# Feature-major x beside token-major x: the first layer's stationary tiles without transposes

## The chip, the cores and the metric

One core of a Trainium2 chip runs the kernel. The metric is the device time of one execution in microseconds, as the median over runs; smaller is better. Engines are named as in the profile: PE (TensorE; PEld its weight loads), DVE (VectorE), ACT (ScalarE), POOL (GpSimd) and SP (SyncE, which here only issues DMAs). POOL issues DMAs too, on a queue of its own.

## The reference

256 tokens of width 2048 pass through two blocks of two layers each, in float32. Only the start of the first block's first layer matters here:

```python
def hybrid_layer(x, layer_idx, norm_gain, w_in, ...):
    h = rms_norm(x, norm_gain)                      # x * rsqrt(mean(x^2) + eps) * gain
    proj = jnp.einsum('bsd,de->bse', h, w_in)       # 256x2048 @ 2048x20480
    (da_q, da_k, da_v, da_z, sb_q, sb_k, sb_v, sb_z, gate_a, gate_b) = split_columns(proj)
    q = rope(rms_norm(da_q.reshape(b, s, 2 * DA_HEADS, DA_QK_DIM), qk_q_gain))
    k = rope(rms_norm(da_k.reshape(b, s, 2 * DA_HEADS, DA_QK_DIM), qk_k_gain))
    ...                                             # two attentions, gated branches
    return x + jnp.einsum('bsd,de->bse', y, w_out)
```

The second block (a convolution, a windowed attention and a linear recurrence per layer) and everything after the first half unit of the first layer keep their instructions.

## The kernel before, in words

**Products.** Every large matrix product is made in three fp32r matmuls (hi times hi, lo of the weight, lo of the activation: lines 1955 to 1957). The weights stream from HBM once, in halves of 128 x 1024 float32 (512 KB). A half lands in one of the `RING = 4` slots of `raw`; ACT copies it to `w_hi` (line 663), DVE subtracts to `w_lo` (line 1181) and counts `split_ready`, and PE multiplies it, 12 matmuls of 512 columns for a half. I call the half with number s *weight half s* and its twelve matmuls *product s*. Eight halves make a unit of 512 output columns: products 0 to 7 fill accumulators 0 and 1, products 8 to 15 fill 2 and 3, product 16 starts the next unit. ACT may overwrite a slot of `w_hi` only when the product four back is done; SP issues the load into a slot of `raw` when `split_ready` says that the half four back was split (line 463).

**The stationary side.** `hT` holds x times the norm gain, feature-major, as hi and lo. The row factor rsqrt(mean x^2) is not in it; it is applied to the accumulators afterwards. x comes token-major in eight parts of 256 KB, 256 features each (`x_part`, line 449). For part f, PE turns four 128x128 squares with `turn_h` (line 1981) into PSUM `work`, ACT writes `hT` hi (`h_hi`, line 682) and DVE `hT` lo (`h_lo`, line 1187). In the first layer PE warms up with six matmuls on zeros (line 1990), turns parts 0 and 1, and then turns part s + 2 behind product s.

**Queues.** Each engine does its instructions in program order. SP issues: x part 0, the identity (`cst`, 64 KB), `kept` (18 KB: norm gains), then weight halves 0 to 3 alternating with x parts 1 to 4, then x parts 5 to 7, then the weight halves from 4 on as slots come free. POOL waits until all x parts are there, then issues the other constants (`cst`, 704 KB), `par` (640 KB) and the rotary tables `ropeC` and `ropeS` (256 KB each).

**What follows in the first step.** On ACT, `first_step` splits halves 8 and 9, squares x over whole rows (line 711, two instructions with a row sum each; their output goes to the scratch `rows`), splits halves 10 and 11, and then waits for POOL's row factor (`x_rstd`) before it takes the first unit's q and k out of the accumulators (`evac_qk`, line 737). On POOL, `layer_start` multiplies the tables by the gains (line 504), waits for the sums of squares and makes the row factor (lines 483 and 489); then `rotate` squares, scales and rotates q and k into `QN` (lines 515 to 533). On PE, `turn_qk` (line 2018) stands behind product 16 and waits for `QN`.

Of the kernel before, what the change touches and what calls it, by code (L numbers as in the profile page):

```python
# [28 lines left out]
ACT = mybir.ActivationFunctionType  # L29
# [142 lines left out]
        return [self.sem(f"{name}{i}") for i in range(n)]  # L172


def build_program(nc, weights, x_in, consts1, params1, kept1, rope1, meta_in, ln_in, consts2, params2,
                  mats2, rows2, out):
    with ExitStack() as ctx:
        mem = Memory(nc, ctx)
# [31 lines left out]
        SM = mem.place("SM", [P, 2, 384])  # L210
        MX = mem.place("MX", [P, 2, 384])
        rows = mem.place("rows", [P, NT, D], at=rows_at)
        pair_at = mem.at
        TZ = mem.place("TZ", [P, NT, 256])
        ZG = mem.place("ZG", [P, NT, 256])
# [32 lines left out]

        x_loaded = sems("x_loaded", 8)
        set_loaded, cst_loaded, par_loaded = sem("set_loaded"), sem("cst_loaded"), sem("par_loaded")
        first_hi, first_lo = sem("first_hi"), sem("first_lo")
        const_set, scale_due = sem("const_set"), sem("scale_due")
# [98 lines left out]
        post_delta, post_ss, post_var, post_sub, post_mul = (  # L353
            sem(n) for n in ("post_delta", "post_ss", "post_var", "post_sub", "post_mul"))
        norm_root, norm_rs, post_sqsum = sem("norm_root"), sem("norm_rs"), sem("post_sqsum")
        out_copied, out_copied2, out_stored = sem("out_copied"), sem("out_copied2"), sem("out_stored")

        def conv_tap(eng, l, ch, j):

# [85 lines left out]
        @block.sync  # L445
        def _(sp):
            def x_part(f):
                c = slice(256 * f, 256 * f + 256)
                sp.dma_start(X[:, :, c], x_in[:, c].rearrange("(t p) n -> p t n", p=P)).then_inc(x_loaded[f], 16)

            x_part(0)
            sp.dma_start(cst[:, C_ID:C_ID + P], consts1[:, C_ID:C_ID + P]).then_inc(set_loaded, 16)
            sp.dma_start(kept[:, :, :], kept1).then_inc(set_loaded, 16)
            for slot in range(RING):
                sp.dma_start(raw[:, slot, :], weights[slot]).then_inc(raw_loaded[slot], 16)
                x_part(slot + 1)
            for f in range(RING + 1, 8):
                x_part(f)
            with sp.Fori(1, n_halves // RING) as r:
                for slot in range(RING):  # L460

                    sp.wait_ge(split_ready, RING * r + (slot + 1 - RING))
                    sp.dma_start(raw[:, slot, :], weights[bass.ds(RING * r + slot, 1), :, :].rearrange("a p n -> p (a n)"))\
                      .then_inc(raw_loaded[slot], 16)

            for n, (t, j) in enumerate(OUT_ORDER):
                sp.wait_ge(out_copied2, n + 1)
                sp.dma_start(out[t * P:t * P + P, columns_of(j)], out_rows[:, t, columns_of(j)]).then_inc(out_stored, 16)
            sp.wait_ge(out_stored, 8 * 16)
# [3 lines left out]
        def _(pool):  # L473
            pool.memset(half_neg, -0.5).then_inc(const_set, 1)
            for f in range(8):
                pool.wait_ge(x_loaded[f], 16)
            pool.dma_start(cst[:, P:C_COLS], consts1[:, P:C_COLS]).then_inc(cst_loaded, 16)

            def scale(*operands):

# [10 lines left out]
            def layer_start(l):  # L491

                pool.wait_ge(y_ready, 4 * l)
                pool.dma_start(par[:, :], params1[l]).then_inc(par_loaded, 16)
                pool.dma_start(ropeC[:, :, :, :], rope1[0]).then_inc(par_loaded, 16)
                pool.dma_start(ropeS[:, :, :, :], rope1[1]).then_inc(par_loaded, 16)
                pool.wait_ge(const_set, 2)
                pool.wait_ge(par_loaded, 48 * (l + 1))
                pool.wait_ge(set_loaded, 32)

                for t in range(NT):
                    for c, table in enumerate((ropeC, ropeS)):
                        gains = par[:, R_QK + 2 * P * c:R_QK + 2 * P * (c + 1)].rearrange("p (a n) -> p a n", a=2)
                        pool.tensor_tensor(table[:, t, :, :], table[:, t, :, :], gains, ALU.mult).then_inc(tables_ready, 1)
                scale(subln[:, :], par[:, R_SUBLN:R_SUBLN + 256], kept[:, l, KC + 1:KC + 2], None,
                                   ALU.mult).then_inc(tables_ready, 1)
                pool.wait_ge(x_ss, 2 * (l + 1))
                rsqrt_mean(rstdx, ssx, x_tmp, D, tables_ready, 6 * (l + 1), x_rstd)
                pool.wait_ge(x_rstd, 2 * l + 1)
                scale(half_rstdx, rstdx, 0.5, None, ALU.mult).then_inc(x_rstd, 1)  # L510
# [138 lines left out]
        def _(act):  # L649
# [27 lines left out]
                act.activation(w_hi[:, slot, :], raw[:, slot, :], ACT.Copy).then_inc(hi_ready, 1)  # L677

            def h_hi(l, f):
                act.wait_ge(hT_turned, 8 * l + f + 1)  # L680
                for c in (2 * f, 2 * f + 1):
                    ins = act.activation(hT[0][:, c, :], work[:, f % 4, c % 2 * SEQ:(c % 2 + 1) * SEQ], ACT.Copy,
                                         scale=kept[:, l, c:c + 1])
                ins.then_inc(hT_hi, 1)

            def layer_start(l):
                u = UNITS1 * l
                if l == 0:
                    act.wait_ge(const_set, 2)
                    act.activation(small[:, 90:91], U[:, 0, 0:1], ACT.Copy)  # L690
                    act.wait_ge(set_loaded, 32)
                    act.wait_ge(raw_loaded[0], 16)
                    act.activation(w_hi[:, 0, 0:512], raw[:, 0, 0:512], ACT.Copy).then_inc(first_hi, 1)
                    h_hi(l, 0)
                    act.activation(w_hi[:, 0, 512:HALF], raw[:, 0, 512:HALF], ACT.Copy).then_inc(hi_ready, 1)
                    for f in range(1, 8):
                        split(u, f, f + 1)
                        h_hi(l, f)
                else:
                    split(u, 0, 6)  # L700
                    h_hi(l, 6)
                    h_hi(l, 7)
                    split(u, 6, 8)

            def first_step(m):
                l = m["l"]
                u = UNITS1 * l
                split(u, 8, 10)
                act.wait_ge(x_added, 4 * l)
                for t in range(NT):  # L710
                    act.activation(rows[:, t, :], X[:, t, :], ACT.Square, accum_out=ssx[:, t:t + 1]).then_inc(x_ss, 1)
                split(u, 10, 12)
                act.wait_ge(x_rstd, 2 * l + 2)
                evac_qk(m)
                split(u, 12, 14)
                act.wait_ge(lam_dots, 2 * (l + 1))
                act.activation(lam_exp, lam_dot, ACT.Exp).then_inc(lam_exps, 1)
                if l == 0:
                    act.wait_ge(cst_loaded, 16)
                    act.activation(tri[:, :], cst[:, C_NEGTRI:C_NEGTRI + 2 * P], ACT.Copy)  # L720
                split(u, 14, 16)
# [452 lines left out]
        def _(dve):  # L1174
# [9 lines left out]
            def h_lo(l, f):  # L1184
                dve.wait_ge(hT_hi, 8 * l + f + 1)
                for c in (2 * f, 2 * f + 1):
                    ins = dve.scalar_tensor_tensor(  # L1187
                        hT[1][:, c, :], work[:, f % 4, c % 2 * SEQ:(c % 2 + 1) * SEQ],
                        kept[:, l, c:c + 1], hT[0][:, c, :], ALU.mult, ALU.subtract)
                ins.then_inc(hT_lo, 1)  # L1190

            def layer_start(l):
                u = UNITS1 * l
                if l == 0:
                    dve.memset(U[:, :, :], 0.0).then_inc(const_set, 1)
                    dve.wait_ge(set_loaded, 32)
                    dve.wait_ge(first_hi, 1)
                    dve.tensor_tensor(w_lo[:, 0, 0:512], raw[:, 0, 0:512], w_hi[:, 0, 0:512], ALU.subtract).then_inc(first_lo, 1)
                    h_lo(l, 0)
                    dve.wait_ge(hi_ready, 1)  # L1200
                    dve.tensor_tensor(w_lo[:, 0, 512:HALF], raw[:, 0, 512:HALF], w_hi[:, 0, 512:HALF], ALU.subtract)\
                        .then_inc(split_ready, 1)
                    for f in range(1, 8):
                        split(u, f, f + 1)
                        h_lo(l, f)
                else:
                    split(u, 3, 6)
                    h_lo(l, 6)
# [733 lines left out]
        def _(pe):  # L1942
# [26 lines left out]

            def turn_h(l, f):  # L1970

                if l:
                    pe.wait_ge(x_added, 4 * (l - 1) + f // 2 + 1)
                else:
                    pe.wait_ge(x_loaded[f], 16)
                if f >= 4:
                    pe.wait_ge(hT_lo, 8 * l + (f - 3))
                for c in (2 * f, 2 * f + 1):
# [5 lines left out]
            def first_step(m):  # L1984
                l = m["l"]
                u = UNITS1 * l
                if l == 0:
                    pe.wait_ge(const_set, 2)
                    for _ in range(FIRST_WARM):
                        pe.matmul(work[:, 3, 0:256], U[:, 0, 0:P], U[:, 1, :], start=True, stop=True)  # L1990
                    pe.wait_ge(set_loaded, 32)
                    turn_h(l, 0)
                    turn_h(l, 1)

                pe.wait_ge(qk_evac, m["n"])
                for s in range(8):
                    halves(u, hT, s, s + 1, (hT_lo, 8 * l), l == 0 and s == 0)
                    if l == 0 and s < 6:
                        turn_h(l, s + 2)
                    if l and s == 1:  # L2000
                        turn_h(l, 6)
                        turn_h(l, 7)
# [704 lines left out]
```

## Time and profile before

| | before |
|---|---|
| device time, median of 3 runs | 3218.58 us (3218.3 to 3219.7) |
| profiled execution, span from first to last instruction | 3216.8 us |
| PE busy | 3208.1 us |
| DVE, ACT, POOL busy | 2002.6, 1666.2, 502.8 us |
| DMA, mean over the span | 177 GB/s, of 568.95 MB |

The profile is of one execution. Its span stands 1.8 us under the median of the timed runs, and within 0.1% of it. Starts are counted from the first instruction. "Idle before" is the time an engine stood still ahead of an instruction, with what released it; a DMA's "us to landing" counts from its issue until its data is there. PE's matmuls overlap their neighbours, so of two in a row the distance of the starts is what counts.

### The profile page before, as it was taken

Reading aid. Unit: us, or ns where it says so; the run is one execution under the profiler, and the core shown is the slowest. Engines: PE = TensorE matmul, PEld = TensorE weight load, DVE = VectorE, ACT = ScalarE, POOL = GpSimd, SP = SyncE. Lnnn points to the kernel's source line nnn. Section 1 sums busy time; section 2 is a strip of 40 time slices with the busy share of each in tenths; the row PEclk is TensorE's granted clock in tenths of the full one; section 3 lists DMA queues with packets and bytes.
Section 4 is the critical chain, followed back from the end, with each engine's and each line's share of the span. In section 5 each row is a group of like instructions: output and inputs, shape, how many; then the busy total and the mean of one; then the engine's idle time right before and its main releaser. Section 6 shows DMA issues by size and latency. Waiting matters only on the chain.

```text
span 3216.8 us, 47383 instructions
## 1 busy us (share of the span) xinstructions
PE 3208.1 (100%) x16986; PEld 2760.8 (86%) x16986; DVE 2002.6 (62%) x2267; ACT 1666.2 (52%) x2326; POOL 502.8 (16%) x425
## 2 busy tenths in 40 slices
PE   9999999999999999999999999999999999999999
PEld 7888888888888888888888888888889999999997
DVE  6667655555544555666654555444458888688975
ACT  5445455555444444454455555444446557465663
POOL 4544500000000003445410000000001000100000
PEclk9999999999999999999999999999999999999999
DMA  6555555554555555455555455555564444544454
GB/s 241 174 171 183 173 174 169 176 171 168 191 195 192 193 196 185 164 187 171 170 178 179 165 175 174 183 192 194 192 209 166 155 144 147 181 160 162 145 182 146
DMA packets 157289, 568.95 MB, mean 177 GB/s; under 512 B 17552, under 2 KB 19744, under 8 KB 156768
## 3 DMA queue, kind: packets, MB, share of 16 engines
q1 hardware_dynamic: 155680, 558.00, 52.1%
q0 software_dynamic: 1488, 9.26, 0.8%
q8 instruction: 86, 1.41, 0.2%
q14 instruction: 35, 0.29, 0.0%
HBM read 565.09 MB, written 2.10 MB: 176 GB/s over the span
## 4 chain that ended last, share of the span: by engine, by line
PE 99%; POOL 1%; DVE 0%; issue 0%; ACT 0%; DVEq 0%; POOLq 0%; ACTq 0%
PE acc L1955 23%; PE acc L1957 23%; PE acc L1956 23%; PE acc L2343 5%; PE acc L2344 5%; PE acc L2345 5%; PE acc L2270 1%; PE acc L2268 1%; PE acc L2269 1%; PE work L2018 1%; PE work L2406 1%; PE work L2314 1%; PE work L2317 1%; PE work L2318 1%; PE work L2373 0%; PE work L2432 0%
## 5 line engine op out<-in xcount | busy, mean ns | idle before, releaser
L1181 DVE TENSOR_TENSOR w_lo<-raw,w_hi 128x1024 fp32r<-128x1024 f32 x1055 | 1400.2, 1337 | 992.2 <-ACT w_hi L663 858.4
L663 ACT ACTIVATE w_hi<-raw 128x1024 fp32r<-128x1024 f32 x831 | 873.4, 1057 | 903.9 <-PE acc L1957 898.7
L1955 PE MATMUL acc<-w_hi,hT_hi 128*128 128x512 f32 x2560 | 1013.7, 396 | 1.4 <-DVE hT_lo L1187 1.4
L1957 PE MATMUL acc<-w_hi,hT_lo 128*128 128x512 f32 x2560 | 998.1, 390 | 0.0
L1956 PE MATMUL acc<-w_lo,hT_hi 128*128 128x512 f32 x2560 | 996.6, 389 | 0.0
L1957 PEld LDWEIGHTS acc<-w_hi,hT_lo 128*128 128x128 f32 x2560 | 480.5, 188 | 102.6
L1955 PEld LDWEIGHTS acc<-w_hi,hT_hi 128*128 128x128 f32 x2560 | 481.0, 188 | 96.2 <-issue 1.7
L1956 PEld LDWEIGHTS acc<-w_lo,hT_hi 128*128 128x128 f32 x2560 | 481.4, 188 | 95.5
L677 ACT ACTIVATE w_hi<-raw 128x1024 fp32r<-128x1024 f32 x224 | 236.1, 1056 | 260.1 <-PE acc L2345 200.1
L2343 PE MATMUL acc<-h_hi,w_hi 128*128 128x272 f32 (+1 forms) x1088 | 318.5, 293 | 0.0
L2344 PE MATMUL acc<-h_lo,w_hi 128*128 128x272 f32 (+1 forms) x1088 | 311.9, 287 | 0.0
L2345 PE MATMUL acc<-h_hi,w_lo 128*128 128x272 f32 (+1 forms) x1088 | 311.8, 287 | 0.0
L2343 PEld LDWEIGHTS acc<-h_hi,w_hi 128*128 128x128 f32 x1088 | 205.3, 189 | 2.3 <-issue 0.3
L2344 PEld LDWEIGHTS acc<-h_lo,w_hi 128*128 128x128 f32 x1088 | 205.4, 189 | 0.8
L2345 PEld LDWEIGHTS acc<-h_hi,w_lo 128*128 128x128 f32 x1088 | 205.7, 189 | 0.0
L1955 PE MATMUL acc<-w_hi,uaT_hi 128*128 128x512 f32 x512 | 200.8, 392 | 0.0
L1957 PE MATMUL acc<-w_hi,uaT_lo 128*128 128x512 f32 x512 | 199.4, 390 | 0.0
L1956 PE MATMUL acc<-w_lo,uaT_hi 128*128 128x512 f32 x512 | 199.3, 389 | 0.0
L483 POOL TENSOR_SCALAR ZG<-TZ 128x512 f32<-128x512 f32 x32 | 34.3, 1072 | 713.0 <-ACT TZ L731 713.0
L483 POOL TENSOR_SCALAR small<-small 128x8 f32<-128x8 f32 (+2 forms) x64 | 34.2, 534 | 547.7 <-ACT SM L780 339.7
L1957 PEld LDWEIGHTS acc<-w_hi,uaT_lo 128*128 128x128 f32 x512 | 96.1, 188 | 20.2
L1956 PEld LDWEIGHTS acc<-w_lo,uaT_hi 128*128 128x128 f32 x512 | 96.2, 188 | 19.6
(381 smaller groups left out, 3830.4 us busy)
## 6 DMA issues: line engine op xcount, KB each, us to landing
raw<-weights SPq DMA_DIRECT2D x1056, 512.0 KB, 3.4
mat<-mats POOLq DMA_DIRECT2D x2, 1536.0 KB, 8.7
X<-x_in SPq DMA_DIRECT2D x8, 256.0 KB, 8.1
GB_rows<-rows POOLq DMA_DIRECT2D x1, 2048.0 KB, 9.9
out<-out_rows SPq DMA_DIRECT2D x8, 256.0 KB, 2.6
par<-params POOLq DMA_DIRECT2D x2, 640.0 KB, 5.4
cst<-consts POOLq DMA_DIRECT2D x1, 704.0 KB, 6.2
cst<-consts POOLq DMA_DIRECT2D x1, 552.0 KB, 5.1
```

The lines of the kernel that those rows point to most:

```text
L483: return pool.tensor_scalar(*operands)
L663: act.activation(w_hi[:, slot, :], raw[:, slot, :], ACT.Copy).then_inc(hi_ready, 1)
L677: act.activation(w_hi[:, slot, :], raw[:, slot, :], ACT.Copy).then_inc(hi_ready, 1)
L1181: dve.tensor_tensor(w_lo[:, s % RING, :], raw[:, s % RING, :], w_hi[:, s % RING, :], ALU.subtract)\
L1955: pe.matmul(o, stat[0][:, kc, token], hi, start=(kc == 0), stop=False)
L1956: pe.matmul(o, stat[0][:, kc, token], lo, start=False, stop=False)
L1957: ins = pe.matmul(o, stat[1][:, kc, token], hi, start=False, stop=(kc == KC - 1))
L2018: ins = pe.transpose(work[:, a // 2, o:o + P], src[:, t, a, :], ident)
L2268: pe.matmul(o, y_hi, hi, start=False, stop=False, skip_group_check=True)
L2343: pe.matmul(o, hi, x_hi, start=(kc == 0), stop=False)
L2344: pe.matmul(o, hi, x_lo, start=False, stop=False)
L2345: ins = pe.matmul(o, lo, x_hi, start=False, stop=(kc == KC - 1))
```

## The change

x is given twice: as before, and as `xT_in`, the same numbers feature-major. `XT` is a tile for it, 16 KB a partition, at the address of the scratch `rows`. The first layer's `h_hi` and `h_lo` read `XT` in SBUF instead of `work` in PSUM, and the 32 transposes of that layer go. SP's order becomes: XT part 0, `kept`, weight halves 0 to 3 alternating with XT parts 1 to 4, XT parts 5 to 7, and then each of weight halves 4 to 7 with two token-major x parts behind it; from half 8 on it is as before. The identity is no longer loaded by itself: all of `cst` (768 KB) is loaded by POOL, behind `par`, `ropeC` and `ropeS`. POOL waits for the XT parts instead of the x parts. ACT's squares of the first layer wait for all of x and for the last `h_lo`, since they write over `XT`. On ACT and DVE each `h_hi` and `h_lo` comes ahead of the split of the weight half that it goes with, not behind it. The second layer and the second block keep their instructions.

```diff
+        XT = mem.place("XT", [P, KC, SEQ], at=rows_at)
...
-            x_part(0)
-            sp.dma_start(cst[:, C_ID:C_ID + P], consts1[:, C_ID:C_ID + P]).then_inc(set_loaded, 16)
+            def xT_part(f):
+                sp.dma_start(XT[:, 2 * f:2 * f + 2, :], xT_in[:, 2 * f:2 * f + 2, :]).then_inc(xT_loaded[f], 16)
+
+            def load(first, slot):
+                sp.wait_ge(split_ready, first + (slot + 1 - RING))
+                sp.dma_start(raw[:, slot, :], weights[bass.ds(first + slot, 1), :, :].rearrange("a p n -> p (a n)"))\
+                  .then_inc(raw_loaded[slot], 16)
+
+            xT_part(0)
             sp.dma_start(kept[:, :, :], kept1).then_inc(set_loaded, 16)
             for slot in range(RING):
                 sp.dma_start(raw[:, slot, :], weights[slot]).then_inc(raw_loaded[slot], 16)
-                x_part(slot + 1)
+                xT_part(slot + 1)
             for f in range(RING + 1, 8):
-                x_part(f)
-            with sp.Fori(1, n_halves // RING) as r:
+                xT_part(f)
+            for slot in range(RING):
+                load(RING, slot)
+                x_part(2 * slot)
+                x_part(2 * slot + 1)
+            with sp.Fori(2, n_halves // RING) as r:
...
             for f in range(8):
-                pool.wait_ge(x_loaded[f], 16)
-            pool.dma_start(cst[:, P:C_COLS], consts1[:, P:C_COLS]).then_inc(cst_loaded, 16)
+                pool.wait_ge(xT_loaded[f], 16)
...
                 pool.dma_start(ropeS[:, :, :, :], rope1[1]).then_inc(par_loaded, 16)
+                if l == 0:
+                    pool.dma_start(cst[:, :], consts1).then_inc(cst_loaded, 16)
...
             def h_hi(l, f):
-                act.wait_ge(hT_turned, 8 * l + f + 1)
+                if l == 0:
+                    act.wait_ge(xT_loaded[f], 16)
+                else:
+                    act.wait_ge(hT_turned, 8 * (l - 1) + f + 1)
                 for c in (2 * f, 2 * f + 1):
-                    ins = act.activation(hT[0][:, c, :], work[:, f % 4, c % 2 * SEQ:(c % 2 + 1) * SEQ], ACT.Copy,
-                                         scale=kept[:, l, c:c + 1])
+                    src = work[:, f % 4, c % 2 * SEQ:(c % 2 + 1) * SEQ] if l else XT[:, c, :]
+                    ins = act.activation(hT[0][:, c, :], src, ACT.Copy, scale=kept[:, l, c:c + 1])
...
                     for f in range(1, 8):
+                        h_hi(l, f)
                         split(u, f, f + 1)
-                        h_hi(l, f)
...
-                act.wait_ge(x_added, 4 * l)
+                if l:
+                    act.wait_ge(x_added, 4 * l)
+                else:
+                    act.wait_ge(x_loaded, 8 * 16)
+                    act.wait_ge(hT_lo, 8)
...
-                    pe.wait_ge(set_loaded, 32)
-                    turn_h(l, 0)
-                    turn_h(l, 1)
 
                 pe.wait_ge(qk_evac, m["n"])
                 for s in range(8):
                     halves(u, hT, s, s + 1, (hT_lo, 8 * l), l == 0 and s == 0)
-                    if l == 0 and s < 6:
-                        turn_h(l, s + 2)
```

DVE's `h_lo` and its place change in the same way as ACT's `h_hi`.

## Rows read from the trace of the kernel before

**Rows 1.** The page: span, and busy time of each engine.

```profile
span 3216.8 us, 47383 instructions
PE 3208.1 (100%) x16986; PEld 2760.8 (86%) x16986; DVE 2002.6 (62%) x2267; ACT 1666.2 (52%) x2326; POOL 502.8 (16%) x425
```

**Rows 2.** Waits of PE over the span: us in total, times, longest.

```profile
PE work L1990 <- DVE U L1195: 1.5, 1, 1.5
PE acc L1955 <- DVE hT_lo L1187: 1.4, 1, 1.4
PE work L2018 <- POOL QN L533: 1.0, 1, 1.0
```

**Rows 3.** The chain that ended last, 28 to 64 us: start, us, what.

```profile
28.61 0.45 PE work L1981 x4
...
29.92 1.89 ACT w_hi L663 x2
31.82 0.06 ACT rows L711
...
37.00 0.92 POOL small L483
...
60.01 1.09 PE work L2018 x8
```

**Rows 4.** Timeline, SP and POOL issues: start, us, what, idle before.

```profile
1.24 0.46 SPq L452 DMA_DIRECT2D cst<-consts  x1
2.22 0.43 SPq L455 DMA_DIRECT2D raw<-weights  x1
...
5.42 0.49 SPq L455 DMA_DIRECT2D raw<-weights  x1
...
17.79 0.68 POOL L477 DMA_DIRECT2D cst<-consts  x1 [16.94 <-DMA X<-x_in]
...
22.84 0.33 SPq L463 DMA_DIRECT2D raw<-weights  x1
```

**Rows 5.** DMA issues, us to landing: weight halves 0, 3 and 9.

```profile
raw<-weights SPq DMA_DIRECT2D x1, 512.0 KB, 4.1
raw<-weights SPq DMA_DIRECT2D x1, 512.0 KB, 8.7
raw<-weights SPq DMA_DIRECT2D x1, 512.0 KB, 6.9
```

**Rows 6.** DMA totals of two stretches: 0 to 10, then 10 to 28 us.

```profile
DMA packets 1488, 2.25 MB, mean 225 GB/s; under 512 B 242, under 2 KB 1155, under 8 KB 1488
DMA packets 2873, 7.15 MB, mean 397 GB/s; under 512 B 264, under 2 KB 1527, under 8 KB 2872
```

**Rows 7.** Timeline, DVE and ACT, splits of weight halves 0 and 1.

```profile
7.17 0.69 DVE L1198 TENSOR_TENSOR w_lo<-raw,w_hi 128x512 fp32r<-128x512 f32 x1 [5.76 <-ACT w_hi L693]
9.33 1.06 ACT L663 ACTIVATE w_hi<-raw 128x1024 fp32r<-128x1024 f32 x1 [0.23 <-DMA raw<-weights]
10.42 1.23 DVE L1181 TENSOR_TENSOR w_lo<-raw,w_hi 128x1024 fp32r<-128x1024 f32 x1 [0.33 <-ACT w_hi L663]
```

**Rows 8.** Timeline, PE: warm-up, products 0 and 1, a later matmul pair.

```profile
1.46 5.49 PE L1990 MATMUL work<-U 128*128 128x256 f32 x12 [1.46 <-DVE U L1195]
9.59 0.47 PE L1955 MATMUL acc<-w_hi,hT_hi 128*128 128x512 f32 x1 [1.45 <-DVE hT_lo L1187]
...
12.19 0.40 PE L1957 MATMUL acc<-w_hi,hT_lo 128*128 128x512 f32 x1
...
12.78 0.47 PE L1955 MATMUL acc<-w_hi,hT_hi 128*128 128x512 f32 x1
...
66.42 0.59 PE L2026 MATMUL work<-QT 128*128 128x256 f32 x2
```

**Rows 9.** Timeline, POOL: first multiplication of the tables, start of the row factor.

```profile
29.09 0.74 POOL L504 TENSOR_TENSOR ropeC<-ropeC,par 128x256 f32<-128x256 f32 x1 [9.01 <-issue]
...
35.80 0.19 POOL L483 TENSOR_SCALAR small<-small 128x2 f32<-128x2 f32 x1 [0.98 <-ACT rows L711]
```

More of the change, by code:

```diff
@@ L172, in sems, with build_program @@
         return [self.sem(f"{name}{i}") for i in range(n)]
-def build_program(nc, weights, x_in, consts1, params1, kept1, rope1, meta_in, ln_in, consts2, params2,
+def build_program(nc, weights, x_in, xT_in, consts1, params1, kept1, rope1, meta_in, ln_in, consts2, params2,
                   mats2, rows2, out):
@@ L241, in build_program @@
         assert mem.at <= 229376, mem.at
-        x_loaded = sems("x_loaded", 8)
+        xT_loaded, x_loaded = sems("xT_loaded", 8), sem("x_loaded")
         set_loaded, cst_loaded, par_loaded = sem("set_loaded"), sem("cst_loaded"), sem("par_loaded")
@@ L355, in build_program @@
         norm_root, norm_rs, post_sqsum = sem("norm_root"), sem("norm_rs"), sem("post_sqsum")
-        out_copied, out_copied2, out_stored = sem("out_copied"), sem("out_copied2"), sem("out_stored")
+        out_copied2, out_stored = sem("out_copied2"), sem("out_stored")
         def conv_tap(eng, l, ch, j):
@@ L448, in x_part @@
                 c = slice(256 * f, 256 * f + 256)
-                sp.dma_start(X[:, :, c], x_in[:, c].rearrange("(t p) n -> p t n", p=P)).then_inc(x_loaded[f], 16)
-            x_part(0)
-            sp.dma_start(cst[:, C_ID:C_ID + P], consts1[:, C_ID:C_ID + P]).then_inc(set_loaded, 16)
+                sp.dma_start(X[:, :, c], x_in[:, c].rearrange("(t p) n -> p t n", p=P)).then_inc(x_loaded, 16)
+            def xT_part(f):
[5 more added lines that the diff above has]
+            xT_part(0)
             sp.dma_start(kept[:, :, :], kept1).then_inc(set_loaded, 16)
@@ L455, in _ @@
                 sp.dma_start(raw[:, slot, :], weights[slot]).then_inc(raw_loaded[slot], 16)
-                x_part(slot + 1)
+                xT_part(slot + 1)
             for f in range(RING + 1, 8):
-                x_part(f)
-            with sp.Fori(1, n_halves // RING) as r:
+                xT_part(f)
[4 more added lines that the diff above has]
+            with sp.Fori(2, n_halves // RING) as r:
                 for slot in range(RING):
-                    sp.wait_ge(split_ready, RING * r + (slot + 1 - RING))
-                    sp.dma_start(raw[:, slot, :], weights[bass.ds(RING * r + slot, 1), :, :].rearrange("a p n -> p (a n)"))\
-                      .then_inc(raw_loaded[slot], 16)
+                    load(RING * r, slot)
             for n, (t, j) in enumerate(OUT_ORDER):
@@ L496, in layer_start @@
                 pool.dma_start(ropeS[:, :, :, :], rope1[1]).then_inc(par_loaded, 16)
+                if l == 0:
+                    pool.dma_start(cst[:, :], consts1).then_inc(cst_loaded, 16)
                 pool.wait_ge(const_set, 2)
                 pool.wait_ge(par_loaded, 48 * (l + 1))
-                pool.wait_ge(set_loaded, 32)
+                pool.wait_ge(set_loaded, 16)
                 for t in range(NT):
@@ L690, in layer_start @@
                     act.activation(small[:, 90:91], U[:, 0, 0:1], ACT.Copy)
-                    act.wait_ge(set_loaded, 32)
+                    act.wait_ge(set_loaded, 16)
+                    h_hi(l, 0)
                     act.wait_ge(raw_loaded[0], 16)
                     act.activation(w_hi[:, 0, 0:512], raw[:, 0, 0:512], ACT.Copy).then_inc(first_hi, 1)
-                    h_hi(l, 0)
                     act.activation(w_hi[:, 0, 512:HALF], raw[:, 0, 512:HALF], ACT.Copy).then_inc(hi_ready, 1)
                     for f in range(1, 8):
+                        h_hi(l, f)
                         split(u, f, f + 1)
-                        h_hi(l, f)
                 else:
@@ L1186, in h_lo @@
                 for c in (2 * f, 2 * f + 1):
-                    ins = dve.scalar_tensor_tensor(
-                        hT[1][:, c, :], work[:, f % 4, c % 2 * SEQ:(c % 2 + 1) * SEQ],
-                        kept[:, l, c:c + 1], hT[0][:, c, :], ALU.mult, ALU.subtract)
+                    src = work[:, f % 4, c % 2 * SEQ:(c % 2 + 1) * SEQ] if l else XT[:, c, :]
+                    ins = dve.scalar_tensor_tensor(hT[1][:, c, :], src, kept[:, l, c:c + 1], hT[0][:, c, :], ALU.mult, ALU.subtract)
                 ins.then_inc(hT_lo, 1)
@@ L1195, in layer_start @@
                     dve.memset(U[:, :, :], 0.0).then_inc(const_set, 1)
-                    dve.wait_ge(set_loaded, 32)
+                    dve.wait_ge(set_loaded, 16)
+                    h_lo(l, 0)
                     dve.wait_ge(first_hi, 1)
                     dve.tensor_tensor(w_lo[:, 0, 0:512], raw[:, 0, 0:512], w_hi[:, 0, 0:512], ALU.subtract).then_inc(first_lo, 1)
-                    h_lo(l, 0)
                     dve.wait_ge(hi_ready, 1)
@@ L1203, in layer_start @@
                     for f in range(1, 8):
+                        h_lo(l, f)
                         split(u, f, f + 1)
-                        h_lo(l, f)
                 else:
@@ L1970, in turn_h @@
             def turn_h(l, f):
[L1972 to L1975, printed above, removed]
+                pe.wait_ge(x_added, 4 * (l - 1) + f // 2 + 1)
                 if f >= 4:
@@ L2686 @@
         "x_in": a["x"][0],
+        "xT_in": a["x"][0].reshape(SEQ, KC, P).transpose(2, 1, 0),
         "consts1": stack1_consts(),
```

## The prediction

> **What bounds the kernel now.** I read the page first. PE is busy for 3208.1 of 3216.8 us [rows 1], so only 8.7 us of the span can be taken from its pauses, and everything else has to come out of its own instructions. The list of PE's waits says where the pauses are: three in the whole execution, all in the first 60 us: 1.5 us before the warm-up, 1.4 us before product 0 (for `hT` lo), and 1.0 us at `turn_qk` for `QN` from POOL [rows 2]. Behind that third one PE waits for nobody until the end. So the question for any edit of the start is a single one: when does PE get past `turn_qk`, at 60.0 us now? A shift there moves the end one to one.
>
> The chain of waits answers what sets the 60.0 us, and it is not PE. Followed from 28.6 us, it leaves PE at the transposes of x part 7, goes to ACT (`hT` hi of part 7, then the splits of weight halves 8 and 9, 29.92 to 31.81 us), to ACT's squares of x at 31.82, to POOL's row factor, done at 37.9, through `evac_qk` and the rotation to `QN`, and back to PE at 60.01 [rows 3]. From the start of the squares to `turn_qk` this is 28.2 us of ACT, POOL and DVE work, none of which the change touches. PE reaches `turn_qk` at 59.0 and waits 1.0.
>
> Third, the DMA totals: from 10 to 28 us the queues moved 7.15 MB at 397 GB/s; in the 10 us before that, 2.25 MB at 225 GB/s [rows 6]. The start of this kernel fills the DMA engines until weight half 9 lands, issued at 22.84 and landing 6.9 us later, at 29.7 [rows 4, 5].
>
> **What is removed.** Six groups of four transposes stood between products. One group costs the distance from the last matmul of product 0 to the first of product 1, 12.78 - 12.19 = 0.59 us, less the 0.23 us that two matmuls of a product stand apart: 0.36 us, so 2.2 us for six. The first two groups stood ahead of product 0, which now waits only for weight half 0 and `hT` of part 0. Half 0 landed at 2.22 + 4.1 = 6.3 us [rows 4, 5] and its first 512 columns were split at 7.17 + 0.69 = 7.9 [rows 7]; the identity's issue ahead of it took 0.5 us of SP's time [rows 4] and goes, so 7.4. Product 0 starts at 7.4 instead of 9.59 [rows 8], 2.2 us earlier. With weights always at hand PE would be 4.4 us ahead: product 5 done at 7.4 + 6 x 2.73 = 23.8 us, product 7 at 29.2 (12 matmuls by 0.2275 us are 2.73).
>
> **What is added.** 2.10 MB. x is still loaded whole, and XT comes ahead of it. Both stand before weight half 8 on SP's queue, and none of it is in a gap: the stretch to 28 us is full. The cost of the eight x parts, from two sides: at the full rate, 2.10 MB / 397 GB/s = 5.3 us; by what x parts took, weight half 3 landed at 5.42 + 8.7 = 14.1 [rows 4, 5], and POOL, which waits for the last x part, went on at 17.79 [rows 4], so four parts behind it took at most 3.7 us, 0.9 each, 7.2 for eight. I take the middle, 6.2. Against it stand two gains. An XT part has rows of 2 KB where an x part has 1 KB; the trace shows no such transfer, it lies between the x part (0.9 us) and the full rate (0.66 us for 256 KB), so eight save 0 to 1.9 us; I take 0.8. And weight half 0 is issued 0.5 us earlier, of which I take 0.4. Weight half 9, which landed at 29.7, then lands at 29.7 + 6.2 - 0.8 - 0.4 = 34.7 us. The lower bound is 29.7 + 5.3 - 1.9 - 0.5 = 32.6, and if the whole slow start to 10 us should go faster as well (2.25 MB at 397 GB/s take 5.7 us, and the first data can't land before 3 us; at most 1.9 us gained), 30.7. The upper bound is 29.7 + 7.2 = 36.9.
>
> **Where it lands in the chain.** ACT takes its instructions in order: split 8, split 9, squares. Split 9 needs the half: 34.7 + 1.06 [rows 7] + 0.1 = 35.9 us, where the squares started at 31.82. They start 4.1 us later, bounds 0.0 and +6.3. The freeing of `w_hi` by product 5, and the two new waits of the squares, are met before: the last x part stands ahead of half 8 on the queue and `hT` lo of part 7 needs only XT. The 28.2 us behind are the same instructions; POOL's times depend on what DVE does beside them, for which I allow 1 us either way. `QN` is ready at 35.9 + 28.1 = 64.0, PE passes `turn_qk` at 64.1.
>
> PE itself is not late for that. Half 8 lands about 1.3 us (512 KB at the full rate) ahead of half 9, at 33.4; with 1.06 us of ACT and 1.23 of DVE [rows 7] product 8 starts at about 35.8. Half 10 is split behind the squares, which costs some 0.5 us, so product 16 ends at 35.8 + 9 x 2.73 + 0.5 = 60.9, over 3 us before `QN`. What the transposes gave is lost there: PE stands for about 4 us before product 8 and 3 us before `turn_qk`.
>
> **The moved constants.** `par` and the tables are now first on POOL's queue, `cst` last with 64 KB more. POOL starts issuing about 1.3 us earlier than 17.79 (0.8 for the rows of XT, 0.5 for the identity's issue). The tables were multiplied from 29.09 us, and POOL then stood 0.98 us for the squares' sums, which came at 35.8 [rows 9]. With x in the same queues `par` and tables may come 1 or 2 us later; cover is there, since the sums come 4 us later: 0. `cst` is needed by PE before product 8; it is issued ahead of half 8 and would land ahead of it. Cost 0, and if it came behind half 9, product 8 would wait until 34.8 instead of 35.8, nothing either. The order of `h_hi` before its split, and reading SBUF instead of PSUM: 0.4 us instructions on engines that now wait for DMAs: 0.
>
> **Sum.** +4.1 us at `turn_qk`, nothing later: the span 3216.8 goes to 3220.9. The median was 1.8 us above the profiled span, so the time is 3218.6 + 4.1 = 3222.7 us. A measurement of this kernel can't tell less than about 0.2%, 6.4 us, from no change: it would be called the same from 3212.1 to 3225.0.
>
> **Rivals.**
> *The load is absorbed (faster).* If weight half 9 landed before 30.7 us, the squares would not move later, and the earlier PE would count. At best split 9 waits for product 5 only (23.8), squares from 24.9 to 28.7; then POOL's tables bind: issued 1.3 us earlier and without `cst` ahead (704 KB, 1.8 us), they are multiplied from 29.1 - 3.1 = 26.0, and what took from 29.1 to 37.9, less the 0.98 us of waiting [rows 3, 9], ends at 33.8, 4.1 us earlier. Time 3214.5. For it: DMA moved only 225 GB/s in the first 10 us. Against: 18 us at 397 GB/s follow, and the absorbed 2.10 MB would need 5.3 us free in them. Chance of this side, down to 3214.5: 0.10.
> *x parts are dear (slower).* From half 0 to half 3 (6.3 to 14.1 us) three halves and three x parts landed; three halves at full rate are 3.9 us, which leaves 1.3 us for an x part. At that price eight cost 10.4; half 9 lands at 29.7 + 10.4 - 1.2 = 38.9, the squares come 8.3 us late, 3226.9. The first microseconds after the ramp look different from the rest, where 0.9 is a ceiling. Chance 0.12.
> *PE's clock falls in the new pause.* The twelve warm-up matmuls took 0.457 us each; a later pair of the same width took 0.59 for both, 0.21 between starts [rows 8]. So PE began at 1.2 GHz for about 6 us and then ran at 2.4, though the granted clock is shown as 1.00 throughout. If it fell back in the 4 us before product 8 and stayed so for another 6 us, PE would lose 3 us, and reach `turn_qk` at 63.9, just hidden; a second fall in the pause there is not hidden, 3 us more: 3225.7. Against: after 1.45 us of pause product 0 ran at full speed, but no row shows a pause of 3 or 4. Chance 0.08.
> The Trainium skill bears on this rival (TensorE: Matmul & The Clock Gate, part 1): an array left idle goes back to 1.2 GHz and needs sustained work to be released. The trace agrees for the start; no row shows it for a pause. By that rule the time is the rival's 3225.7 if both pauses are long enough.
>
> **How the numbers follow.** The forecast, squares late by weight half 9, has 0.70, with 3222.7 and bounds 3218.6 - 1 and 3224.9 + 1. My range is 3217.2 to 3226.4: it leaves out most of the first rival and half of the second. Over 3225.0 lie the second and third rival in part and the forecast's upper edge, 0.13; under 3212.1 only what I have no row for, 0.02; between them 0.85.
>
> **What would show it.** Product 0 near 7.4 us; PE waiting for DVE's `w_lo`, and behind it DMA, before product 8 and perhaps some earlier ones; ACT's split 9 idle for `raw`, landing near 34.7; squares at 35.9; DMA near 400 GB/s until 34; `turn_qk` near 64.1 with a wait for `QN` near 3 us. Wrong would be squares at or before 31.8, a wait on `cst` or on the tables at the end of POOL's chain, or a pause of PE after 65 us.

## The result, and the profile after

| | before | changed |
|---|---|---|
| device time, median of 19 runs each | 3218.36 us (3217.68 to 3219.70) | 3224.17 us (3222.67 to 3226.80) |
| profiled execution, its own time and span | 3218.58, 3216.8 us | 3226.80, 3225.0 us |
| PE busy in the span | 3208.1 us | 3207.0 us |

The ratio is 1.0019, with a 95% interval from 1.0012 to 1.0025. By the medians the change costs 5.8 us. That is under the 0.2% that I had set as the bound, so by it the kernels are the same, but the loss is clear of 1. The profiled execution of the changed kernel happens to be the slowest of its 19.

PE's waits over the span of the changed kernel, us in total, times, longest (before: [rows 2]):

```profile
PE acc L1971 <- DVE w_lo L1198: 6.2, 3, 3.0
PE work L2026 <- POOL QN L543: 3.7, 3, 2.4
PE acc L1971 <- DVE w_lo L1215: 1.8, 1, 1.8
PE work L2003 <- DVE U L1211: 1.5, 1, 1.5
```

Lines 1971 to 1973 are now the products, 1198 the split on DVE, 2026 `turn_qk`. Before, PE lost 3.9 us to waits; now it loses 13.2, and the 2.2 us of transposes that went don't pay for it. The waits for `w_lo` are new and those for `QN` have grown. The timeline of PE shows where the long ones are (start, us, what, idle before and its releaser):

```profile
7.58 0.47 PE L1971 MATMUL acc<-w_hi,hT_hi 128*128 128x512 f32 x1 [1.82 <-DVE w_lo L1215]
12.54 0.47 PE L1971 MATMUL acc<-w_hi,hT_hi 128*128 128x512 f32 x1 [2.00 <-DVE w_lo L1198]
27.59 0.47 PE L1971 MATMUL acc<-w_hi,hT_hi 128*128 128x512 f32 x1 [1.16 <-DVE w_lo L1198]
33.63 0.47 PE L1971 MATMUL acc<-w_hi,hT_hi 128*128 128x512 f32 x1 [3.04 <-DVE w_lo L1198]
65.15 1.34 PE L2026 MATMUL work<-cst,QN 128*128 128x128 f32 x8 [2.41 <-POOL QN L543]
```

Product 0 starts at 7.58 instead of 9.59 [rows 8]. Product 1 then waits for its weights, product 6 waits, product 7 waits 3.0 us, and `turn_qk` starts at 65.15 us, 5.1 us later than before. What DVE had waited for is on ACT, in its timeline:

```profile
31.17 1.06 ACT L673 ACTIVATE w_hi<-raw 128x1024 fp32r<-128x1024 f32 x1 [4.19 <-DMA raw<-weights]
33.88 1.06 ACT L673 ACTIVATE w_hi<-raw 128x1024 fp32r<-128x1024 f32 x1 [1.66 <-DMA raw<-weights]
35.12 1.06 ACT L673 ACTIVATE w_hi<-raw 128x1024 fp32r<-128x1024 f32 x1 [0.18 <-DMA raw<-weights]
36.09 1.89 ACT L728 ACTIVATE rows<-X 128x2048 f32<-128x2048 f32 x1
```

These are the splits of weight halves 7, 8 and 9, each of them as the half lands, and behind them the squares, at 36.09 us instead of 31.82 [rows 3]. The issues and landings of halves 7 and 9, from the timeline of SP and the DMA issues:

```profile
16.33 1.23 SPq L457 DMA_DIRECT2D raw<-weights  x1
24.14 1.75 SPq L457 DMA_DIRECT2D raw<-weights  x1
```

```profile
raw<-weights SPq DMA_DIRECT2D x1, 512.0 KB, 14.8
raw<-weights SPq DMA_DIRECT2D x1, 512.0 KB, 11.0
```

The first of each pair is half 7, the second half 9. Half 9 lands at 24.14 + 11.0 = 35.1 us, where it landed at 29.7 before [rows 4, 5]. From 10 to 28 us the DMA totals are

```profile
DMA packets 3388, 7.06 MB, mean 392 GB/s; under 512 B 293, under 2 KB 1867, under 8 KB 3388
```

which is the same full stretch as before [rows 6]; it now goes on to 33 us. The chain of waits behind the landing (start, us, what) has the order of before [rows 3]:

```profile
24.14 10.96 DMA raw<-weights
...
37.98 2.00 ACT rows L728 x2
...
41.36 0.92 POOL small L491
...
58.91 3.26 POOL QN L539
...
62.25 2.77 POOL QN L543
...
65.15 1.34 PE work L2026 x8
```

One thing in it is longer: from the squares' start to `turn_qk` it takes 29.1 us, where it was 28.2. Line 539, the sum into `QN`, takes 3.26 us; in the profile before the same step took 2.39. POOL and DVE work side by side there, and their instructions meet at other moments than before; that this is the reason is likely, but no run tests it. And one thing is not in the chain at all. The stretches of 2 us around the two long pauses (us, PE, PEld, DVE, ACT, POOL busy, granted clock, DMA share, GB/s):

```profile
32.00:34.00 2.00, 0.37 (x2) 0.36 (x3) 1.23 (x1) 0.34 (x2) 0.00 (x0) 1.00 0.86 341
34.00:36.00 2.00, 2.00 (x9) 1.59 (x8) 1.02 (x1) 1.82 (x2) 0.00 (x0) 0.78 0.76 236
36.00:38.00 2.00, 2.00 (x6) 1.55 (x5) 1.43 (x2) 2.00 (x4) 0.00 (x0) 0.50 0.48 133
38.00:40.00 2.00, 2.00 (x9) 1.60 (x8) 0.00 (x0) 2.00 (x4) 0.00 (x0) 0.87 0.89 315
...
64.00:66.00 2.00, 0.85 (x7) 0.86 (x8) 2.00 (x1) 0.00 (x0) 2.00 (x2) 0.96 0.71 246
66.00:68.00 2.00, 2.00 (x8) 1.61 (x7) 0.09 (x1) 1.09 (x2) 1.86 (x2) 0.50 0.41 109
68.00:70.00 2.00, 2.00 (x8) 1.57 (x7) 0.00 (x0) 0.00 (x0) 1.28 (x1) 0.69 0.45 178
```

The granted clock fell to 0.50, its lower level of 1.2 GHz, behind both pauses. It did not fall with the pause but after PE had gone on: product 7 starts at 33.63, and from 35.09 us its matmuls start 0.43 us apart instead of 0.23. The first time that costs PE its lead and nothing else; the second time nothing is left to hide it. The price is read from the next `turn_qk`, that of the second step, in the timelines of the kernel before and of the changed one:

```profile
108.01 1.03 PE L2018 MATMUL work<-cst,QN 128*128 128x128 f32 x8
114.78 1.03 PE L2026 MATMUL work<-cst,QN 128*128 128x128 f32 x8
```

They are 6.8 us apart, where the first were 5.1 apart: 1.6 us for the clock. The missing 1.3 us of the profiled 8.2 are the two other waits for `QN`, 0.6 us near 1380 and 0.7 near 1430 us, in the second layer, whose code is the same. Why they came in this execution is not shown; one such wait, of 0.6 us, stands in the second layer of a variant of the kernel before too (squares early, below).

### The profile page after: what moved, and what is told of

Same layout as the page of the kernel before. It is cut to its first block, busy times and chain, and to the rows that moved or that the text cites. A ratio compares the mean times of both kernels' runs of the same rounds, so it can differ in the third digit from the quotient of the medians.

```text
span 3225.0 us, 47309 instructions
## 1 busy us (share of the span) xinstructions
PE 3207.0 (99%) x16954; PEld 2758.3 (86%) x16954; DVE 1996.5 (62%) x2267; ACT 1667.6 (52%) x2326; POOL 503.6 (16%) x425
## 4 chain that ended last, share of the span: by engine, by line
PE 96%; POOL 2%; DMA 1%; issue 0%; DVE 0%; SPq 0%; ACT 0%; DVEq 0%; POOLq 0%; ACTq 0%
PE acc L1971 23%; PE acc L1973 23%; PE acc L1972 23%; PE acc L2351 5%; PE acc L2352 5%; PE acc L2353 5%; PE acc L2278 1%; PE acc L2276 1%; PE acc L2277 1%; PE work L2026 1%; DMA raw<-weights 1%; PE work L2414 1%; PE work L2322 1%; PE work L2325 1%; PE work L2326 1%; PE work L2381 0%
```

## The experiments

Each time is set against the kernel before, timed beside it on the same chip: 3218.11 us for the first four experiments, 3218.15 for the next four, 3218.45 for the last.

**Late x.** The 2.10 MB leave the start.

```diff
             for slot in range(RING):
                 load(RING, slot)
-                x_part(2 * slot)
-                x_part(2 * slot + 1)
+            # ... halves 8 to 19 ...
+            for slot in range(RING):
+                load(RING * 5, slot)
+                x_part(2 * slot)
+                x_part(2 * slot + 1)
...
-                    act.activation(rows[:, t, :], X[:, t, :], ACT.Square, accum_out=...)
+                    act.activation(rows[:, t, :], X[:, t, :] if l else XT[:, 8 * t:8 * t + 8, :]..., ACT.Square, accum_out=...)
```

> The changed kernel, with the token-major x parts moved behind weight halves 20 to 23. The first layer's squares read XT in their place (so the row factor, and with it the output, is another one; instructions and sizes are the same). Theory, that the 2.10 MB in front of weight half 9 hold back the squares: half 9 lands near 29 us, the squares start when product 5 has let go of w_hi, near 27 us or soon after half 9, PE reaches turn_qk near 56 to 57 us after one pause of 2 us before product 1, and nothing makes it wait long: 3 to 4 us under the kernel before, 3214 to 3216 us. Rival, that XT itself (the order of h_hi ahead of the split, the SBUF reads, rows of 2 KB) costs: squares stay later than 31.8 us and the time over 3218. Rival, that PE's clock in the pauses is the cost: the same low time, since there is no pause to lower it, but with the squares still near 36 us.

Measured: 3219.54 us (ratio 1.0004, 0.9995 to 1.0013), 1.4 us over the kernel before and 4.4 us less of a loss than the change has. The squares start at 30.29 us (36.09 in the changed kernel), so the bytes are what holds them back. But the expected gain did not come, and the profile says why: half 9 still landed only at 29.3, the squares were still behind it, and the chain from them to `turn_qk` took 29.2 us as in the changed kernel. So `turn_qk` started at 59.46, half a microsecond earlier than before, after PE had waited

```profile
PE work L2032 <- POOL QN L548: 3.4, 1, 3.4
```

and the clock fell at the end of that wait, in these two stretches:

```profile
58.00:60.00 2.00, 0.54 (x3) 0.55 (x4) 2.00 (x1) 0.00 (x0) 2.00 (x2) 0.69 1.07 391
60.00:62.00 2.00, 2.00 (x9) 1.88 (x8) 0.40 (x1) 0.54 (x2) 1.92 (x2) 0.50 1.04 365
```

So there are two causes: the bytes, and the clock. An earlier PE alone gained nothing; by the medians it lost 1.4 us, with an interval that holds 1.

**The bytes alone.** The kernel before, with eight XT parts behind halves 4 to 7 that nobody reads.

```diff
             for slot in range(RING):
                 load(RING, slot)
+                xT_part(2 * slot)
+                xT_part(2 * slot + 1)
```

> The kernel before with its transposes and order, and the 2.10 MB alone added: eight parts of XT, which nobody reads, behind weight halves 4 to 7. Theory: half 9 lands 5 to 6 us later than 29.7, the squares start near 36.5 us, turn_qk near 65, and PE's clock falls in a pause before product 7 or 8 and again before turn_qk: 3223 to 3226 us, the same as the changed kernel or a little over. Rival, that the changed kernel's loss comes from its new waits and order and not from the bytes: within 1 us of the kernel before.

Measured: 3222.72 us (1.0014, 1.0005 to 1.0023), 4.6 us over the kernel before. ACT's timeline has the squares at

```profile
36.53 1.89 ACT L724 ACTIVATE rows<-X 128x2048 f32<-128x2048 f32 x1
```

4.7 us later than before, and `turn_qk` starts at 64.81 after a wait of 0.31 us. Of the two expected falls of the clock one came: PE waited 3.6 us before product 7 and the clock was 0.50 from 38 to 40 us, which brought PE later to `turn_qk`, where it would have waited in any case. Before `turn_qk` there was no pause to speak of and no fall. The rival is dead: with the old order and the old waits, the bytes give four fifths of the loss.

**Filling the pause.** The changed kernel with matmuls on zeros ahead of the first `turn_qk`.

```diff
+                for _ in range(fill):          # 5 in the second step of the first layer, else 0
+                    pe.matmul(work[:, 3, 0:256], U[:, 0, 0:P], U[:, 1, :], start=True, stop=True)
                 if prev:
                     turn_qk(prev)
```

> The changed kernel with five matmuls on zeros (256 columns, as in the warm-up) behind product 16 and ahead of turn_qk in the second step of the first layer alone, which is taken out of its loop for that; they fill 2.15 of the 2.4 us in which PE waits for QN. Theory, that the lower clock behind that pause costs 1.6 us on top of the late squares: no fall at 66 us, 1.3 to 1.7 us under the changed kernel, 3222.5. Rival, that the clock costs nothing in the time, being hidden by a later wait: no difference, 3224.2. Squares, QN and turn_qk stay where they are, at 36.1, 65.0 and 65.1 us.

Measured: 3223.05 us (1.0015, 1.0006 to 1.0024), 4.9 us over the kernel before where the changed kernel is 5.8 over. The granted clock is 1.00 from 58 to 70 us, and `turn_qk` is late as ever, with the next one 48.0 us behind it as in the kernel before (49.6 in the changed one):

```profile
64.64 1.09 PE L2028 MATMUL work<-cst,QN 128*128 128x128 f32 x8
...
66.00:68.00 2.00, 2.00 (x10) 1.62 (x9) 0.00 (x0) 0.86 (x2) 1.84 (x3) 1.00 0.60 227
```

The direction is the expected one, the size 0.9 to 1.1 us instead of 1.3 to 1.7, and the intervals of the two ratios overlap. It may be that not every execution of the changed kernel lost as much to the clock as the profiled one; that can't be read from times alone.

**Squares first.** The changed kernel with the squares ahead of splits 8 and 9.

```diff
-                split(u, 8, 10)
+                if l:
+                    split(u, 8, 10)
...
-                split(u, 10, 12)
+                split(u, 10 if l else 8, 12)
```

> The changed kernel with the first layer's squares ahead of the splits of weight halves 8 and 9 on ACT. Theory, that the end is set by squares, row factor, rotation: the squares start behind the split of half 7 near 32.3 us, 3.8 us earlier, QN is ready near 61.3; product 8 waits for its split until 38.5, so PE reaches turn_qk near 63 us and there is no long pause and no lower clock there: 3 us under the changed kernel, 3220.5 to 3222. Rival, that weight halves on PE set the end: the splits of 8 and 9 come 3.8 us later and the time is the changed kernel's or up to 4 us more.

Measured: 3222.39 us (1.0012, 1.0003 to 1.0021), 4.3 us over the kernel before. `QN` was ready at 61.9, but PE reached `turn_qk` at 65.02 without a wait. It had lost what `QN` had won:

```profile
38.79 0.47 PE L1971 MATMUL acc<-w_hi,hT_hi 128*128 128x512 f32 x1 [2.21 <-DVE w_lo L1198]
```

```profile
38.00:40.00 2.00, 1.21 (x4) 1.00 (x5) 2.00 (x3) 2.00 (x3) 0.74 (x1) 0.79 0.11 29
40.00:42.00 2.00, 2.00 (x6) 1.56 (x5) 2.00 (x6) 1.38 (x3) 0.54 (x1) 0.50 1.06 313
```

Product 8 waits for its late split, and behind the pauses before products 7 (3.0 us) and 8 (2.2 us) the clock is at 0.50. I had counted the late split but not the clock, and so expected 63 us. With the 2.10 MB in front, PE and `QN` are both late, and moving the squares only swaps them.

**Squares early in the kernel before.** No new bytes; the squares where ACT is idle, and the constants behind the tables.

```diff
                     for f in range(1, 8):
                         split(u, f, f + 1)
                         h_hi(l, f)
+                        if f in (5, 6):        # at f == 5 behind waits for all x parts
+                            squares(f - 5)
...
-            pool.dma_start(cst[:, P:C_COLS], consts1[:, P:C_COLS]).then_inc(cst_loaded, 16)
...
                 pool.dma_start(ropeS[:, :, :, :], rope1[1]).then_inc(par_loaded, 16)
+                if l == 0:
+                    pool.dma_start(cst[:, P:C_COLS], consts1[:, P:C_COLS]).then_inc(cst_loaded, 16)
```

> The kernel before with two edits and no new bytes: the first layer's squares stand behind the hT of x parts 5 and 6 on ACT, where it is idle for 1.4 us a step and x is complete, and the constants but for the identity are loaded behind the tables. Theory, that turn_qk is set by squares, row factor and rotation: the row factor is done near 35.2 us (bound by the tables on POOL), QN near 57.3, PE reaches turn_qk at 59.0 without a wait: 1.0 us under the kernel before, 3217.1, and nothing more, since PE is then the bound. Rival, that PE's own start (transposes, pause before product 0) is what counts: no difference.

Measured: 3217.58 us (0.9999, 0.9990 to 1.0008), 0.6 us under the kernel before by the medians, not told from no difference by its interval. The row factor was done at 32.5 us, and now `evac_qk` waits for product 7:

```profile
31.53 0.95 POOL L482 TENSOR_SCALAR small<-small 128x2 f32<-128x2 f32 x1 [0.20 <-POOL small L488]
36.74 1.90 POOL L516 TENSOR_TENSOR SQ<-QK 128x1024 f32<-128x1024 f32 x1 [4.26 <-ACT QK L747]
```

`turn_qk` starts at 58.67 without a wait (`QN` was ready at 58.2). That is 1.3 us earlier than before, of which the profiled execution kept 0.4: a wait for `QN` of 0.6 us stands between 1500 and 1600 us, in the second layer. So in the kernel before, PE and POOL's chain are within about a microsecond of each other, and an edit on one of them alone can win little more than that.

**The constants behind the tables.** This part of the change alone, on the kernel before.

> The kernel before with one part of the change alone: the constants (704 KB, the identity stays where it was) are loaded behind par and the tables. The tables are multiplied some 1.8 us earlier and POOL waits that much longer for the squares: no difference, within 0.3 us of the kernel before. Rival: the order of the constants has a part in the loss, 0.5 us or more to either side.

Measured: 3218.46 us (1.0001, 0.9992 to 1.0010), 0.3 us from the kernel before. POOL multiplies the tables from 24.66 us and then waits 5.5 us for the squares. Within what the interval can tell, this part costs nothing in the kernel before.

**Late x, filled.** The first experiment with seven matmuls on zeros ahead of `turn_qk`.

> The run with the token-major x parts late (squares reading XT, so another row factor), with seven matmuls on zeros ahead of turn_qk, 3.0 of the 3.4 us in which PE waits there. Theory, that the early PE gave nothing because QN is not earlier, and that the clock falling in the longer pause cost 2 us more: turn_qk near 59.5 as there and no lower clock behind it, 1.5 to 2.5 us under that run, 3217 to 3218. Rival, that its time over the kernel before comes from somewhere later: no difference.

Measured: 3217.76 us (0.9999, 0.9990 to 1.0008), against its kernel before 1.8 us less than without the filling (-0.4 instead of +1.4). `turn_qk` starts later, at 60.02, and the clock stays:

```profile
60.00:62.00 2.00, 2.00 (x14) 1.79 (x13) 0.32 (x1) 0.90 (x2) 1.92 (x2) 1.00 1.01 372
```

This is the cleaner test of the clock. The two kernels differ in the matmuls on zeros and in a step taken out of its loop for them; `turn_qk` starts 0.56 us later, and the next one 0.8 us earlier (first the kernel without the filling, then with it):

```profile
108.78 1.04 PE L2032 MATMUL work<-cst,QN 128*128 128x128 f32 x8
107.98 1.04 PE L2034 MATMUL work<-cst,QN 128*128 128x128 f32 x8
```

From one `turn_qk` to the next this is 49.3 us without the filling and 48.0 with it. It is 47.9 to 48.0 us in the kernel before and in all experiments but the first, so the fall cost 1.4 us in this profile; the medians are 1.8 us apart.

The same profile has a fall of its own, earlier, behind a pause of 2.1 us before product 1:

```profile
12.00:14.00 2.00, 2.00 (x6) 1.51 (x6) 2.00 (x5) 1.89 (x4) 0.00 (x0) 0.50 1.07 411
```

The profile of the filled pause has one there too, behind 2.0 us (0.50 from 14 to 16 us), while in the changed kernel and in the one with the squares first a pause of 2.0 us at the same place left the clock at 1.00. So the length of a pause alone does not tell whether the clock falls. These falls were hidden, as the first one of the changed kernel was.

**Late x, early squares.** The first experiment with its squares ahead of splits 8 and 9.

> The run with the token-major x parts late (squares reading XT, so another row factor), with the squares ahead of the splits of weight halves 8 and 9: all parts of the wait for QN are moved forward at once. Theory: squares start near 24.5 us, the row factor is done near 32, product 7 near 31, QN near 55, PE passes turn_qk at 55 to 56 us without a pause that lowers the clock: 4 us under the kernel before, 3214. This is what the removed transposes and the earlier product 0 are worth when nothing else stands in the way. Rival, that PE is fed too slowly by the weight halves (halves 8 and 9 landed at 26.6 and 29.3 there): turn_qk at 58 or later.

Measured: 3214.31 us (0.9988, 0.9979 to 0.9997), 3.8 us under the kernel before, the only one whose interval lies below 1. PE's timeline has

```profile
55.62 1.04 PE L2032 MATMUL work<-cst,QN 128*128 128x128 f32 x8
```

without a wait, 4.4 us earlier than before. The next `turn_qk` is 47.9 us behind it. That is the size of the prize when the bytes are gone and both PE and `QN` come forward together; its squares read XT, so it is no version to keep.

**Sums from XT.** A version that computes everything and needs no token-major x at the start.

```diff
+            def square_of_xT(f):               # ACT, behind each split
+                act.activation(XS[:, 2 * f:2 * f + 2, :], XT[:, 2 * f:2 * f + 2, :], ACT.Square)
...
+            def sum_features(s):               # PE: f = s behind products 0 to 3, f = 4 to 7 behind 4
+                pe.matmul(work[:, 3, 0:512], ones, XS[:, 2 * f:2 * f + 2, :]..., start=(f == 0), stop=(f == 7))
+                # behind product 5, from ACT's copy of the sums in TZ:
+                pe.matmul(work[:, 2, t:t + 1], TZ[:, c, t * P:t * P + P], share, start=(c == 0), stop=(c == 1))
```

> The changed kernel with the token-major x parts behind weight halves 20 to 23 and the first layer's sums of squares made from XT: ACT squares each XT part into a free tile (0.5 us each, in its idle time), PE adds over the features with eight matmuls of 512 columns on a tile of ones, ACT copies the sums, PE brings them to the tokens' partitions with four small matmuls, DVE copies them for POOL. It computes all of the reference. Theory, that the run with late x and early squares (3214.3 us, turn_qk at 56) shows what there is to win and the sums' own work on PE (1.9 us for the eight, some 1.2 for the four) is paid out of it, and that the row factor is ready before product 7 ends, near 33.8 us: turn_qk near 58.4, 1.6 us under the kernel before, 3216.5. Rival, that the chain sums, copy, sums, copy comes behind product 7 and holds evac_qk and with it QN: turn_qk at 60 us or later, 3218 or over.

Measured: 3217.19 us (0.9995, 0.9986 to 1.0004), 1.3 us under the kernel before by the medians; its interval holds 1. It is 7 us under the changed kernel, and under the kernel before by less than this measurement can assure. Its `turn_qk` waits for nothing:

```profile
57.50 1.04 PE L2070 MATMUL work<-cst,QN 128*128 128x128 f32 x8
```

The eight sums on PE cost less than 2 us and the four small ones 0.8 (eight instructions from 26.67 to 27.48).

## Why the prediction was right, and where it was not

**PE's three waits decide, and turn_qk is the point where the start is paid.** Right. PE has no pause from 70 us on but two of 0.65 and 0.7 us in the second layer, which are not the change's.

**The removed transposes and the earlier product 0 are lost.** Right. Product 0 came at 7.58 (7.4 predicted). The bytes without the removal cost 4.6 us, with it 5.8: by the medians (the intervals overlap) the removal did not only bring nothing, it cost 1.2 us. That fits the clock, which fell at `turn_qk` in the changed kernel, behind 2.4 us of waiting, and not with the bytes alone, behind 0.3.

**2.10 MB before half 9.** Right in place and in the sum, with some luck in its terms. Half 9 landed at 35.1 (34.7), the squares started at 36.09 (35.9). The bytes alone moved them to 36.53, and without the bytes they were at 30.29. From 30.29 to 36.09 the x parts cost 5.8 us, where I took 6.2; the rows of 2 KB and the earlier start brought 0.4 (half 9 at 29.3 without the x parts, 29.7 before), where I took 1.2. The two errors went against each other. That no part is absorbed holds: the stretch to 28 us ran at 392 GB/s, as before at 397. My lowest bound, 30.7, has a slip: 10 us less 3 less 5.7 leaves 1.3 us to gain and not 1.9, which makes it 31.3; the result lies far from either.

**The order on the queues.** Wrong in a step that cost nothing. I had half 7 landing well ahead of POOL's loads, and PE's long pause before product 8. Half 7 was issued at 16.33, before `par` (17.42, landed 7.6 us later, at 25.0) and the tables, and landed after them at 31.1; so the pause came before product 7. In the kernel before, halves 4 to 7 had gone ahead of POOL's loads. The Trainium skill (DMA: Bandwidth & Descriptors, Queues, rings and completion order) says that each DMA engine goes round between the queues that have work for it; the changed kernel's trace agrees, with a half issued 1.1 us before `par` that landed 6.1 us after it. Half 9, behind everything on both queues, should come at the same time by either order; that would be why the sum held. The tables, which I had 1 or 2 us later, came earlier (27.1 us from 29.1). That is the move of the constants, which alone, in the kernel before, brings them to 24.66; the rest of the change takes 2.4 us of it back.

**28.2 us behind the squares.** Mis-sized by 0.9 us, inside the 1 us allowed for what DVE does beside POOL.

**The clock.** The step that failed. I gave the fall of the clock a chance of 0.08, as a rival to the late squares, with a price of 3 us only if both pauses were long. It was no rival but came on top: after pauses of 3.0 and 2.4 us the clock fell both times, and the second fall cost 1.6 us of the profiled execution, more than any other term that the sum lacked. The first cost PE as much, hidden: nine matmuls from 35.09 us took 3.64 us, where nine at 0.2275 take 2.05. So a fall has half the price that I gave it (3 us). The sum lacked this term, and the median lies 1.5 us over the forecast. The rule that I named (the Trainium skill, TensorE: Matmul & The Clock Gate, part 1) said so; the trace after agrees with it. So do the runs: the same pause filled with matmuls on zeros kept the clock at 1.00 and took 1.8 us off in the one pair, and about 1 us in the other. What I had taken as evidence against it, full speed after 1.45 us of pause, was a shorter pause; but pauses of 2.0 us came out both ways.

**The rivals.** The load was not absorbed, and x parts were not dearer than 0.9 us. Nor did the constants' order cost anything that the run of it alone could show.

What stays open: how the 19 executions split between the clock and POOL's meetings with DVE. Only one was profiled, the slowest; its 8.2 us are accounted for (4.3 squares, 0.9 chain, 1.6 clock, 1.3 second layer), the median's 5.8 are not term by term. Open too is what decides between a pause of 2.0 us that brings the clock down and one that doesn't.

## What to carry to other kernels

When two chains arrive at one point within a microsecond of each other, speeding up one of them is worth no more than that microsecond; find the join and move both. At the start of a kernel, where the DMA queues run full, count the bytes ahead of the last transfer that the critical chain waits for, on all queues together: here 2.10 MB that nobody needed for a millisecond, but for a row sum, cost 4.6 us. And an engine made early waits longer: if it is TensorE, the pause can be paid a second time in its clock, here with 1.4 to 1.6 us behind pauses of 3.4 and 2.4 us.

## What was not expected of the hardware

- With matmuls on zeros in place of the pause before `turn_qk` the granted clock stayed at 1.00 there, in two kernels; without them it went down to 0.50 (for all of 66 to 68 us in the changed kernel). Zeros are enough.
- Over all profiles the clock fell behind pauses of 2.0 to 3.6 us, and did not behind others of 2.0 us and less.
- A transfer issued 1.1 us before another queue's landed 6.1 us behind it (half 7 and `par`); the changed kernel's queues were not served in the order of issue.
- The same chain of some 20 POOL and DVE instructions took from 28.2 to 29.2 us in seven profiles, with single POOL instructions of one shape at 0.74 or 1.72 us.
